# Latent attention: the score matmuls of a step issued in two parts, with values and transposes between them

## The reference

```python
cq = rms_norm_2(h @ w_dq, q_norm)
q = (cq @ w_uq).reshape(b, s, MLA_HEADS, MLA_QK)
...
k = jnp.concatenate([kv[..., :MLA_NOPE], k_rope], axis=-1)
v = kv[..., MLA_NOPE:]
q = rms_norm_2(q, q_gain)
k = rms_norm_2(k, k_gain)
q = jnp.concatenate([q[..., :MLA_NOPE], apply_rope(q[..., MLA_NOPE:], pos)], axis=-1)
k = jnp.concatenate([k[..., :MLA_NOPE], apply_rope(k[..., MLA_NOPE:], pos)], axis=-1)
o = chunk_causal_attention(q, k, v)
...
sc = jnp.einsum('bqhd,bkhd->bhqk', qi, k, preferred_element_type=jnp.float32) * scale
mask = key_chunk[None, :] <= q_chunk[:, None]
p = jax.nn.softmax(jnp.where(mask, sc, -jnp.inf), axis=-1)
return jnp.einsum('bhqk,bkhd->bqhd', p.astype(v.dtype), v)
```

## The kernel before

| engine | step s before |
|---|---|
| PE | T(2s-4), P0 P1 R of step s, T(2s-3), V(2s-5), V(2s-4) |
| ACT | copy(2s-4), exp(2s-2), copy(2s-3), exp(2s-1) |
| DVE | norm(2s-2), max(2s), max(2s+1), norm(2s-1) |

## Time and profile before

### The profile page before, as it was taken

How to read it: one execution, slowest core, us unless ns; L and a number is a source line. 1 busy time by engine, 2 the same in 40 slices (tenths; PEclk the granted TensorE clock), 3 DMA queues, 4 the chain that set the end, 5 groups by cost and what they waited for, 6 DMA issues and landing times.

```text
span 2586.1 us, 35264 instructions
## 1 busy us (share of the span) xinstructions
PE 2557.9 (99%) x12636; PEld 2031.6 (79%) x12636; DVE 1661.4 (64%) x2384; ACT 1273.8 (49%) x2129; POOL 360.5 (14%) x270
## 2 busy tenths in 40 slices
PE   9999999999999999999999999999999999999999
PEld 7855788888787557788888775789988777899887
DVE  4476677643988895677653777587633546687533
ACT  4326544333546895444333577567533425567432
POOL 0020100000103781100000130000610002000800
PEclk9999999999999999999999999999999999999999
DMA  5330222222233442222222230132232221232222
GB/s 215 107 93 25 96 98 97 97 98 95 82 135 118 135 131 73 85 98 94 97 98 97 95 103 1 60 120 99 88 107 96 92 104 50 98 123 99 82 97 97
DMA packets 74689, 250.44 MB, mean 97 GB/s; under 512 B 8748, under 2 KB 8876, under 8 KB 74192
## 3 DMA queue, kind: packets, MB, share of 16 engines
q1 hardware_dynamic: 73488, 240.63, 27.1%
q0 software_dynamic: 944, 8.33, 0.9%
q10 hardware_dynamic: 144, 0.00, 0.0%
HBM read 242.50 MB, written 2.24 MB: 95 GB/s over the span
## 4 chain that ended last, share of the span: by engine, by line
PE 90%; DVE 4%; ACT 2%; issue 1%; POOL 1%; SPq 0%; DMA 0%; DVEq 0%; ACTq 0%; POOLq 0%
PE bank L409 25%; PE bank L410 24%; PE bank L411 24%; PE bank L2199 2%; PE bank L1302 2%; PE bank L1304 2%; PE bank L1303 2%; POOL xT L852 1%; DVE mT L477 1%; PE bank L2751 1%; PE bank L3097 1%; PE bank L1647 1%; PE bank L1636 1%; PE bank L2206 1%; ACT arena L2826 0%
## 5 line engine op out<-in xcount | busy, mean ns | idle before, releaser
L383 DVE TENSOR_TENSOR wlo<-wraw,whi 128x1024 fp32r<-128x1024 f32 x349 | 447.7, 1284 | 444.6 <-ACT whi L360 444.0
L360 ACT ACTIVATE whi<-wraw 128x1024 fp32r<-128x1024 f32 x357 | 375.9, 1055 | 497.6 <-DMA wraw<-in_w 497.5
L409 PE MATMUL bank<-hnhi,whi 128*128 128x512 f32 (+1 forms) x1528 | 596.3, 390 | 0.8 <-DVE wlo L383 0.5
L410 PE MATMUL bank<-hnlo,whi 128*128 128x512 f32 (+1 forms) x1528 | 584.5, 382 | 0.0
L411 PE MATMUL bank<-hnhi,wlo 128*128 128x512 f32 x1392 | 542.1, 389 | 0.0
L409 PE MATMUL bank<-ahi,whi 128*128 128x512 f32 x1184 | 463.5, 391 | 1.8 <-DVE stats L2860 0.6
L410 PE MATMUL bank<-alo,whi 128*128 128x512 f32 x1184 | 460.8, 389 | 0.0
L411 PE MATMUL bank<-ahi,wlo 128*128 128x512 f32 x1184 | 460.8, 389 | 0.0
L409 PEld LDWEIGHTS bank<-hnhi,whi 128*128 128x128 f32 x1528 | 287.3, 188 | 85.1 <-issue 29.2
L410 PEld LDWEIGHTS bank<-hnlo,whi 128*128 128x128 f32 x1528 | 287.4, 188 | 57.8 <-issue 3.4
L411 PEld LDWEIGHTS bank<-hnhi,wlo 128*128 128x128 f32 x1392 | 261.3, 188 | 55.2
(11 more groups left out here) (356 smaller groups left out, 3918.8 us busy)
## 6 DMA issues: line engine op xcount, KB each, us to landing
wraw<-in_w SPq DMA_DIRECT2D x410, 512.0 KB, 3.3
arena<-cs_scratch SPq DMA_DIRECT2D x20, 512.0 KB, 6.0
over_a<-cs_scratch SPq DMA_DIRECT2D x12, 512.0 KB, 6.6
arena<-in_rpb POOLq DMA_DIRECT2D x1, 2880.0 KB, 14.0
out_dram<-xT SPq DMA_DIRECT2D x8, 256.0 KB, 2.0
arena<-in_t_step POOLq DMA_DIRECT2D x2, 897.0 KB, 4.7
mT<-arena SPq DMA_DIRECT2D x28, 64.0 KB, 2.0
arena<-in_t_ab POOLq DMA_DIRECT2D x1, 1472.0 KB, 6.6
```

What stands on the lines that cost most here:

```text
L360: act.activation(whi[:, slot * BLOCK:(slot + 1) * BLOCK], wraw[:, slot * BLOCK:(slot + 1) * BLOCK], ACT.Copy).then_inc(sem("w_hi"), 1)
L383: dve.tensor_tensor(low_home(i), wraw[:, slot * BLOCK:(slot + 1) * BLOCK], whi[:, slot * BLOCK:(slot + 1) * BLOCK], ALU.subtract).then_inc ...
L409: pe.matmul(out, wh, ah, start=start, stop=False)
L410: pe.matmul(out, wh, al, start=False, stop=False)
```

## The change

On PE, `scores` is divided. `plain_scores(s, 0)` issues P0 and waits only for max(2s-2), the reader of the two banks it writes. `plain_scores(s, 1)` issues P1 and waits for max(2s-1), and `rope_scores(s)` issues R as before. The new order of a step is P0, V(2s-6), T(2s-4), P1, R, T(2s-3), V(2s-5). On ACT the first exponentials come ahead of the last copy of values. On DVE the rotary parts of keys 6 and 7 go behind the softmax work up to its step 3.

```diff
-            def scores(s):
+            def plain_scores(s, x):
...
-                    pe.wait_ge(sem("item_max"), n0 + 2 * s)
+                    pe.wait_ge(sem("item_max"), n0 + 2 * s - 1 + x)
                 pe.wait_ge(sem("head_normed"), 2 * g + 2)
-                for x in range(2):
-                    for e in range(2):
-                        lo, hi = rows(e)
-                        pe.matmul(bank[2 * x + e][:, 0:w], q_plain(2 * g + x, lo, hi)[:, c:c + P],
-                                  k_plain(2 * g + x, lo, hi)[:, 0:w], start=True, stop=False)
+                for e in range(2):
+                    lo, hi = rows(e)
+                    pe.matmul(bank[2 * x + e][:, 0:w], q_plain(2 * g + x, lo, hi)[:, c:c + P],
+                              k_plain(2 * g + x, lo, hi)[:, 0:w], start=True, stop=False)
+
+            def rope_scores(s):
...
+            if s < 16:
+                plain_scores(s, 0)
+            if s >= 3:
+                values(2 * s - 6)
             if 2 <= s <= 17:
                 turn(2 * s - 4)
             if s < 16:
-                scores(s)
-            for j, lo, hi in {16: ((0, 0, 2),), 17: ((0, 2, 4),), 18: ((1, 2, 4),)}.get(s, ()):
+                plain_scores(s, 1)
+                rope_scores(s)
+            for j, lo, hi in {16: ((0, 0, 2),), 17: ((0, 2, 4), (1, 0, 2)), 18: ((1, 2, 4),)}.get(s, ()):
                 pe_row(pe, "mla_o", j, lo, hi)
             if 2 <= s <= 17:
                 turn(2 * s - 3)
             if s >= 3:
                 values(2 * s - 5)
-            if s == 17:
-                pe_row(pe, "mla_o", 1, 0, 2)
-            if 2 <= s <= 17:
-                values(2 * s - 4)
```

```diff
# act_mla_proj: ahead of read(27), not behind the roots
+                if i == 27:
+                    act_mla_soft(act, (2, 4))
...
-                if i == 27:
-                    act_mla_soft(act, (2, 4))
# dve_mla_proj and dve_mla
-                    dve_key(dve, UNITS[i - 2][1])
+                    dve_key(dve, UNITS[i - 2][1], ("plain", "rope") if i < 26 else ("plain",))
             dve_mla_soft(dve, (1, 2))
-            dve_key(dve, 7)
+            dve_key(dve, 7, ("plain",))
+            dve_mla_soft(dve, (2, 4))
+            dve_key(dve, 6, ("rope",))
+            dve_key(dve, 7, ("rope",))
...
-            dve_mla_soft(dve, (2, 17))
+            dve_mla_soft(dve, (4, 17))
```

More of the change, by code:

```diff
@@ L2745, in scores @@
                 else:
-                    pe.wait_ge(sem("item_max"), n0 + 2 * s)
+                    pe.wait_ge(sem("item_max"), n0 + 2 * s - 1 + x)
                 pe.wait_ge(sem("head_normed"), 2 * g + 2)
-                for x in range(2):
-                    for e in range(2):
-                        lo, hi = rows(e)
-                        pe.matmul(bank[2 * x + e][:, 0:w], q_plain(2 * g + x, lo, hi)[:, c:c + P],
-                                  k_plain(2 * g + x, lo, hi)[:, 0:w], start=True, stop=False)
+                for e in range(2):
[3 more added lines that the diff above has]
+            def rope_scores(s):
+                g, b = s // 4, mla_block(2 * s)
+                w, c = (b + 1) * P, b * P
                 for x in range(2):
```

## The result

The changed kernel took 2602.41 us (median of five runs, 2600.44 to 2605.17) against 2586.92 us before in the same comparison: a ratio of 1.0059, 95% interval 1.0048 to 1.0071. The time lies inside the range on record and 2.4 us above the forecast of 2600. The difference is 15.5 us, against a forecast of 12.2: the forecast started from 2588 us, 1.1 more than the kernel before took here, and that hides part of what it fell short. The profiled execution has a span of 2603.4 us; before it was 2586.1.

The account below looks back on a forecast made before the run. PE was taken as 99% busy, the round near its limit, with a second cycle through ACT and DVE just below. Chain 11.8, keys and exponentials 0, tail 0.4 gave +12.2 us: 2588 to 2600 us, range 2593 to 2609 (8 in 10).

Parts of the forecast that it names:

- The chain through P0: Steps 5 to 15: P0 delays V, T, copy, exp, norm, next maximum; round 20.7 to 25.0 us, +11.8 us altogether.
- The terms of the chain: Steps 8 to 11: copies later by 2.14, 0.94, 1.33 (0.72 comes through), 0.65 us; less 0.1, 4.3 us a round.
- The signs: Steps 8 to 11: round about 25 us, P1 never waits, P0 waits about 1.1 us, DVE not for R.
- One sign of being wrong: A granted clock below 1 within steps 5 to 15 would point to the clock falling too.
- Two readings behind it: PE runs matmuls in order, read from V(17) behind waiting P; V and T (1.4 us or more) cover the second maximum.
- The prices of P0, V and T: PE, widths 128 to 512: P0 0.43 to 1.07 us, V 0.38 to 1.03, T until copy 0.48 to 1.13.
- The switch, rule against row: P0's switch costs 0.22 us a step, by the row; hidden weight loads would give 9.4 instead of 11.8 us.
- Rotary keys and first exponentials: DVE and ACT: 1 to 2 us won ahead of step 3, about as much lost at step 4; value 0.
- Tail: After the steps, T(28) waits for norm(28), a new wait of some 0.4 us: +0.4.
- The clock: No gain counted: step 3's P ran at granted clock 0.72, and waits of that size were expected to remain.
- the third rival: Clock falls too: slow stretches of 1.6 us, in every second step 9 us more (2609), in each 18 (2618); chance 0.14.
- The faster one: Rival: T comes through P0 in time, so waits fill up; -4.8 us, 2583, or 2579 with free switches; chance 0.07.

Follow-up runs that it names:

- changed, 2nd look: The changed kernel run again unaltered, against the kernel before: 2601.85 us, ratio 1.0061; its profiled execution has a span of 2598.3 us.
- changed, 1st look: The changed kernel's first comparison against the kernel before: 2602.41 us, ratio 1.0059; its profiled execution has a span of 2603.4 us.
- the PE part alone: The kernel before with only PE's new order; ACT and DVE keep their old order: 2604.87 us, ratio 1.0065.
- the two parts alone: The kernel before with only the new ACT and DVE orders (first exponentials, rotary keys), PE unchanged: 2587.27 us, ratio 0.9999.
- the spread version: Changed kernel with P0, P1 together behind V(2s-6), T(2s-4), waiting separately, and rotary keys 6, 7 behind norm(9), norm(19): 2581.46 us, ratio 0.9979.
- Split only: Changed kernel with P0 and P1 side by side behind V(2s-6) and T(2s-4), still waiting separately: 2583.0 us, ratio 0.9985.
- norm late: Changed kernel with DVE doing both maxima, max(2s) and max(2s+1), before norm(2s-2); PE's order kept: 2595.33 us, ratio 1.0029.
- the values-only order: Changed kernel with T(2s-4) moved back ahead of P0, only V(2s-6) between P0 and P1: 2593.85 us, ratio 1.0027.

## Why the prediction was right

The table sets the pieces of the attention steps against the sum, in us from P to P.

| piece | before | changed, 2nd look | changed, 1st look | forecast of the difference |
|---|---|---|---|---|
| steps 0 to 5 | 25.68 | 24.83 | 24.83 | 0 |
| steps 5 to 8 | 16.91 | 20.43 | 22.72 | +3.2 |
| steps 8 to 12 | 20.75 | 24.90 | 26.45 | +4.3 |
| steps 12 to 15 | 16.03 | 19.64 | 19.62 | +3.2 |
| step 15 to the first row product | 4.81 | 6.91 | 6.92 | +1.1 and +0.4 |
| sum | 84.18 | 96.71 | 100.54 | +12.2 |

- *The chain through P0.* Right in place and size: the forecast round was 25.0 us, and the round without a stretch at a low clock took 24.90, that of the PE part alone 24.91. It is shown from three sides. Of the 15.5 us, moving T and V back ahead of P0 returns 15, moving norm behind the maxima returns 8, and moving only T returns 9. The first two leave PE's work in a round as it is, 20.4 us.
- *The terms of the chain, one by one.* They were worked out for the end of each step's first maximum, and P before waits for the second, so the pieces of the table that end at steps of different width can't be set against them. The ends of max(14), (16), (18), (20) and (22) can. In the second look they lie 6.24, 5.95, 6.54 and 6.17 us apart, before 4.12, 5.16, 5.94 and 5.52 (the earlier trace rows and, for max(22), the last row below). That is 2.12, 0.79, 0.60 and 0.65 us more; the forecast had 2.14, 0.84 (0.94 less 0.1), 0.72 and 0.65. Over the eleven links from max(8) to max(30) it is 12.4 us, 0.9 of it the stretch at a low clock; the forecast was 11.8. The first five rows are of the second look, the last is of the kernel before.

```profile
1589.65 0.16 DVE L2867 TENSOR_TENSOR stats<-stats,over_hn 128x2 f32<-128x2 f32 x1
...
1595.89 0.16 DVE L2867 TENSOR_TENSOR stats<-stats,over_hn 128x2 f32<-128x2 f32 x1
...
1601.84 0.16 DVE L2867 TENSOR_TENSOR stats<-stats,over_hn 128x2 f32<-128x2 f32 x1
...
1608.38 0.16 DVE L2867 TENSOR_TENSOR stats<-stats,over_hn 128x2 f32<-128x2 f32 x1
...
1614.55 0.16 DVE L2867 TENSOR_TENSOR stats<-stats,over_hn 128x2 f32<-128x2 f32 x1
```

```profile
1607.01 0.16 DVE L2860 TENSOR_TENSOR stats<-stats,over_hn 128x2 f32<-128x2 f32 x1
```

- *The signs.* In the second look P0 waits before every step from 5 to 15 but step 13, 1.08 us in the mean (forecast about 1.1), no P1 waits, and DVE does not wait for R in the round. One sign of being wrong came as well: the granted clock fell below 1 within these steps.
- *Two readings behind it.* That PE keeps its order was read from V(17), which stood behind the waiting P with its operand ready. The bank that V(17) writes was emptied only at 1603.10, 0.07 us before P started, so that row did not show it. The changed kernel does: in its second look copy(12) had ended at 1593.51, PE idled 0.61 us before P0 of step 9 at 1596.11, and V(12), ready since the copy, started at 1596.95. And V and T cover 1.08 us in step 10, not 1.4 or more; with P0 ahead of them it was still enough.
- *The prices of P0, V and T.* P0 of width 512 went from start to next start in 1.05 us (forecast 1.07), V(14) in 0.38 (0.38), and PE was busy 20.41 us in a round (20.4).
- *The switch, rule against row.* The full switch was paid: the rise from 18.83 to 20.41 us of PE work in a round is 1.58, and four times 0.38 is 1.52. The smaller sum, 2.4 us less, that the prediction set beside the opening table of the Trainium skill's "TensorE: Matmul & The Clock Gate" did not come: the weight load of P0 again starts with the matmul and behind its wait, as here in step 10 of the first look (1607.08, P0 at 1607.09). PE was idle ahead of it, with no matmul in flight.

```profile
1607.08 0.30 PEld L2753 LDWEIGHTS bank<-arena 64*128 64x128 f32 x4 [0.78 <-DVE stats L2867]
```

- *Rotary keys and first exponentials.* Forecast 0, and the two parts alone changed nothing that can be measured. By the ends of the maxima the second look had won 1.6 us at max(6) and lost 1.7 at max(8), so the two sides of the account were right too, and the spread version takes part of the loss back. A part of the win may be the stretch at a low clock at step 3, which went (see the clock). (The 0.85 us in the table's first row are there because P0 does not wait for the second maximum.)
- *Tail.* The forecast was 1.1 for the last link and 0.4 for a wait of T(28) for norm(28). The last link, max(28) to max(30), grew by 0.6 us, and from there to the first row product it is 0.81 us in both kernels: the 0.4 did not come. T(28) waited 0.28 us, by the profile for a copy, while the row product still waited for max(31). The 2.1 us of the table hold 1.5 us that P before had waited for the second maximum of step 14. One row product more moved than the text on the change says: that of step 17, (1, 0, 2), now stands ahead of T(31) and V(29). What this is worth was not tried.
- *The clock.* This is the term that was mis-sized, in the step where I counted no change from the clock: the difference of the first look, +16.4 us in the table, is +12.5 in the second, and the 3.8 between them are the two stretches more. With the one at step 12 the clock took 0.9 us of the second look and some 4.7 of the first. I had this as the third rival with a chance of 0.14, as a case of its own with 9 us or more. It is rather part of the forecast case, with one to three stretches in each of the three executions looked at. The stretch at step 3 that I left standing went away (P0 and P1 took 1.13 us each in both looks); with the PE part alone, where the keys stay in their old place, they took 1.44 and 1.64. So the clock's term of zero stood for a loss of up to 4.7 us. The table's difference without any stretch is 11.6 us, close below the forecast of 12.2; that the stretches make the rest of the measured 15.5 is shown only for the executions that were profiled, and inferred for the others. The medians of 2602.4 and 2601.9 lie between the two looks.
- *The rivals.* The faster one asked that T should reach ACT in time; ACT waited for the transposes before the copies throughout. But the gain that it spoke of exists. Split only wins part of it by leaving P0 where it cannot delay T: the round goes to 19.82 us.

Open: why norm late and the values-only order each take 0.8 to 1.0 us a round more than the cycles I worked out for them. In the values-only order transposes wait for a copy to empty their bank, T(14), T(18) and T(20) for 0.37, 0.53 and 0.72 us, and my sum left that out. In norm late T(16) and T(18) wait 0.26 and 1.01 us for norm and P0 of step 11 waits 0.73 for its maximum; that wait for norm was in my sum, so what made the round longer is not shown. Neither was tried by a run.

## What to carry to other kernels

Before hoisting an instruction in an in-order queue, write down what then stands behind its wait, and follow that through the other engines until it comes back to the awaited event. If it comes back within one step, the sum of that loop is the new step time, and it must be compared with the busiest engine's work. Splitting a wait is good where the first half can fill the wait for the second; putting other work between the halves is good only if nothing urgent is in it. A piece of slack work belongs in steps where its engine idles, one piece at a time.

## What the runs showed that I had not expected

The granted clock did not follow from the order of the program and the waits alone. In both looks at the changed kernel PE waited the same times before P0 of steps 5, 8 and 12 (2.25 or 2.26, 1.85, 1.85 us). In one look the clock then fell each time, in the other only after the last. The transposes T(12) of step 8, in the look where it fell there, took 1.97 us against 1.09, the lower of the two levels, 1.2 instead of 2.4 GHz:

```profile
1593.35 0.70 PE L2753 MATMUL bank<-arena 64*128 64x256 f32 x4 [1.85 <-DVE stats L2867]
...
1595.46 1.97 PE L2778 MATMUL bank<-base_t,arena 128*128 128x128 f32 x8
```

A stretch of the kind cost 0.9 to 2.3 us here. The execution with three of them was the slowest of its five, 2605.17 us, the one with one the fastest of its four, 2600.11, so a comparison of two single profiles of such a kernel can be off by some 4 us from this alone.
